# Hybrid pooling and retention trunk on one core: later gate rows as four narrow rows in one bank, biased once and copied to all partitions by DMAs

## The reference

```python
cond = jax.nn.silu(c)
mod = jnp.einsum('bd,sdk->bsk', cond, ada_w[i]) + ada_b[i]
shift_t, scale_t, gate_t = jnp.split(mod[:, 0], 3, axis=-1)
shift_m, scale_m, gate_m = jnp.split(mod[:, 1], 3, axis=-1)
h = modulate(rmsnorm(x, norm_g[i, 0]), shift_t, scale_t)
x = x + gate_t[:, None, :] * y                 # y: pooling or retention of h
h = modulate(rmsnorm(x, norm_g[i, 1]), shift_m, scale_m)
x = x + gate_m[:, None, :] * sq_relu_mlp(h, mlp_w1[i], mlp_w2[i])
```

## Time and profile before

| | |
|---|---|
| time, median of 3 runs | 2412.22 us (2411.78 to 2412.8) |
| span of the profiled execution | 2411.1 us |
| matmuls | 10401 records; PE 2338.8 us busy |
| weights and other data read from DRAM | 616.26 MB |
| mean DMA rate | 257 GB/s |

### The profile page before, as it was taken

One profiled execution on the slowest core, in us unless ns is written; L12 is line 12 of the kernel. 1 busy time (PEld: TensorE's weight loads), 2 busy tenths in 40 slices (PEclk: granted clock), 3 DMA queues, 4 the chain that ended last, 5 costly groups with the idle time before them and its releaser, 6 DMA issues.

```text
span 2411.1 us, 28969 instructions
## 1 busy us (share of the span) xinstructions
PE 2338.8 (97%) x10401; PEld 1856.6 (77%) x10401; DVE 1581.6 (66%) x1655; ACT 1087.5 (45%) x1354; POOL 22.2 (1%) x32
## 2 busy tenths in 40 slices
PE   6689999999999999999999999999999999999998
PEld 2146788888888887878888888887888888888886
DVE  4578887776786787656566657566876545445455
ACT  2324554544534545444444444445543443443443
POOL 0000000000000000000000000000000000000000
PEclk9799999999999999999999999999999999999999
DMA  9999988898888876776667776766986656656654
GB/s 391 405 408 373 335 315 325 308 312 271 299 305 277 300 260 218 239 224 218 218 225 230 237 224 219 225 219 199 333 289 228 187 189 193 185 190 192 188 185 151
DMA packets 269147, 620.28 MB, mean 257 GB/s; under 512 B 19064, under 2 KB 19400, under 8 KB 268112
## 3 DMA queue, kind: packets, MB, share of 16 engines
q1 hardware_dynamic: 267520, 612.44, 75.1%
q0 software_dynamic: 880, 5.77, 0.7%
q10 hardware_dynamic: 608, 0.22, 0.0%
HBM read 616.26 MB, written 2.10 MB: 256 GB/s over the span
## 4 chain that ended last, share of the span: by engine, by line
PE 88%; DMA 5%; DVE 4%; issue 1%; ACT 1%; SPq 0%; POOL 0%; ACTq 0%; POOLq 0%; DVEq 0%
PE acc L556 83%; DMA ada_early_h<-in_ada_w 3%; PE tb L655 2%; DMA raw<-in_mlp_w 1%; DVE ada_acc L1352 1%; DVE w_lo L1346 1%; PE mod_ps L691 1%; DMA ada_raw<-in_ada_w 0%; PE score_ps L905 0%; ACT w_hi L971 0%; PE score_ps L691 0%; SPq L408 0%; DVE h_lo L1540 0%; PE acc L915 0%; PE acc L916 0%
## 5 line engine op out<-in xcount | busy, mean ns | idle before, releaser
L1346 DVE TENSOR_TENSOR w_lo<-raw,w_hi 128x1024 fp32r<-128x1024 f32 x776 | 947.2, 1225 | 724.2 <-ACT w_hi L971 723.8
L971 ACT ACTIVATE w_hi<-raw 128x1024 fp32r<-128x1024 f32 x776 | 821.8, 1060 | 1147.4 <-PE acc L556 1080.9
L556 PE MATMUL acc<-w_hi,h_lo 128*128 128x512 f32 x1792 | 705.6, 394 | 11.9 <-DVE h_lo L1540 5.7
L556 PE MATMUL acc<-w_hi,h_hi 128*128 128x512 f32 x1792 | 698.0, 389 | 0.0
L556 PE MATMUL acc<-w_lo,h_hi 128*128 128x512 f32 x1792 | 697.4, 389 | 0.0
L556 PE MATMUL acc<-w_hi,a_lo 128*128 128x512 f32 x1312 | 516.9, 394 | 0.0
L556 PE MATMUL acc<-w_hi,a_hi 128*128 128x512 f32 x1312 | 511.2, 390 | 0.0
L556 PE MATMUL acc<-w_lo,a_hi 128*128 128x512 f32 x1312 | 511.2, 390 | 0.0
L556 PEld LDWEIGHTS acc<-w_hi,h_lo 128*128 128x128 f32 x1792 | 336.5, 188 | 87.5 <-issue 10.0
L556 PEld LDWEIGHTS acc<-w_hi,h_hi 128*128 128x128 f32 x1792 | 336.4, 188 | 70.6
L556 PEld LDWEIGHTS acc<-w_lo,h_hi 128*128 128x128 f32 x1792 | 336.7, 188 | 69.1 <-issue 1.4
(11 more groups left out here) (164 smaller groups left out, 761.0 us busy)
## 6 DMA issues: line engine op xcount, KB each, us to landing
raw<-in_mlp_w SPq DMA_DIRECT2D x512, 512.0 KB, 4.3
ada_raw<-in_ada_w SPq DMA_DIRECT2D x280, 512.0 KB, 6.0
raw<-in_ret_w_in SPq DMA_DIRECT2D x192, 512.0 KB, 3.9
ada_early_h<-in_ada_w SPq DMA_DIRECT2D x84, 512.0 KB, 13.1
raw<-in_ret_w_out SPq DMA_DIRECT2D x64, 512.0 KB, 4.3
ada_early_a<-in_ada_w SPq DMA_DIRECT2D x20, 512.0 KB, 9.4
raw<-in_pool_w SPq DMA_DIRECT2D x8, 512.0 KB, 13.1
x<-in_x SPq DMA_DIRECT2D x2, 1024.0 KB, 9.8
```

Source lines behind the costliest of these rows:

```text
L556: mm = nc.tensor.matmul(acc[pair][t][:], l[:, CK * c + j, tok], w[:, c % RING, j, :], start=first and j == 0 and i == 0, stop=last and j = ...
L971: nc.scalar.activation(w_hi[:, o % RING], raw[:, o % RING], ACT.Copy).then_inc(hi_ready, 1)
L1346: nc.vector.tensor_tensor(w_lo[:, o % RING], raw[:, o % RING], w_hi[:, o % RING].bitcast(F32), ALU.subtract).then_inc(lo_ready, 1)
```

## The change

A gate of the three is now summed like a shift or scale: `row_sum` after chunk 1 of unit 7, four blocks of 32 columns in `mod_ps`. The bias is loaded by POOL into four rows of `seg_row` (8 KB), DVE adds the bank to `seg_row` once after chunk 3 (128 x 512), and POOL issues four DMAs that each copy one row of `seg_row` (512 floats in partition 0, 32, 64 or 96) to all 128 partitions of a quarter of the target. The waits follow: ACT's next copy to `seg_row`, `mlp_block` in the last group, and the head of `retention()` wait for the copies (`gate_in`, 64 per gate); PE's next sum and the fills of the two banks at a boundary wait for the biased row.

```diff
@@ PE
-            def gate_blocks(b0):
-                if b0 == 0:
-                    pe.wait_ge(ada_done, n.of("AD"))
...
-                pe.wait_ge(gate_ready, n.of("GB"))
-                for b in (b0, b0 + 1):
-                    nc.tensor.matmul((mod_ps, score_ps)[b % 2][:], ones[:], ada_acc[:, b * NB:(b + 1) * NB],
-                                     start=True, stop=True).then_inc(gate_mm, 1)
-                n.add(GB=2)
+            def gate_row_sum():
+                row_sum()
+                n.add(GR=1)
                             if what == "gate" and u == 7:
-                                hooks[1] = [lambda: gate_blocks(0)]
-                                hooks[5] = [lambda: gate_blocks(2)]
+                                hooks[1] = [gate_row_sum]
@@ fill and row_sum, PE
-                    pe.wait_ge(gate_ready, n.of("GB"))
+                    pe.wait_ge(gate_biased, n.of("GR"))
@@ copy_rows, ACT
+                if n.n["GR"]:
+                    act.wait_ge(gate_in, 64 * n.n["GR"])
@@ DVE
-            def take_gate(b0, target, loaded, loads):
-                dve.wait_ge(loaded, 16 * loads)
-                for b in (b0, b0 + 1):
...
-                    nc.vector.tensor_tensor(target[:, blk], (mod_ps, score_ps)[b % 2][:], target[:, blk],
-                                            ALU.add).then_inc(gate_ready, 1)
+            def take_gate_row():
+                dve.wait_ge(row_bias_in, 16 * (n.n["GR"] + 1))
+                dve.wait_ge(row_mm, n.of("RM") + 1)
+                nc.vector.tensor_tensor(seg_row[:], mod_ps[:], seg_row[:], ALU.add).then_inc(gate_biased, 1)
+                n.add(GR=1, RM=1)
                             if what == "gate" and u == 7:
...
-                                hooks[2] = [lambda at=at: take_gate(0, *at)]
-                                hooks[5] = [lambda at=at: take_gate(2, *at)]
+                                hooks[3] = [take_gate_row]
                             if u >= 4 and not last and (layer, first) != (0, 0):
+                                if first == 3 and u == 4:
+                                    dve.wait_ge(gate_in, 64 * (2 * layer + 1))
                                 mlp_block(u % 2, u - 4, first == 0, first == 3)
             def retention():
-                dve.wait_ge(gate_ready, n.of("GB"))
+                dve.wait_ge(gate_in, 64 * 2)
@@ POOL
-            def load_gate_bias(target, norm_, loaded):
-                row = gate_bias[3 * norm_ + 2:3 * norm_ + 3, :].to_broadcast([P, D])
-                pool.dma_start(target, row).then_inc(loaded, 16)
+            def load_gate_bias(norm_, columns):
+                pool.wait_ge(col_T, columns)
+                pool.dma_start(seg_row[0:P:32, :], gate_bias[3 * norm_ + 2].rearrange("(b n) -> b n", b=4)).then_inc(row_bias_in, 16)
+            def spread_gate(target, rows_before):
+                pool.wait_ge(gate_biased, rows_before + 1)
+                for b in range(4):
+                    pool.dma_start(target[:, b * NB:(b + 1) * NB],
+                                   seg_row[32 * b:32 * b + 1, :].rearrange("p (o n) -> p o n", o=1).to_broadcast([1, P, NB])).then_inc(gate_in, 16)
             pool.wait_ge(h_ready, CH)
-            load_gate_bias(mlp_gate, 1, mlp_bias_in)
+            load_gate_bias(1, 4)
+            spread_gate(mlp_gate, 0)
             pool.wait_ge(part_sum, 6 * TT)
-            load_gate_bias(gate[:], 2, ret_bias_in)
+            load_gate_bias(2, 6)
+            spread_gate(gate, 1)
             tile_roots()
...
             pool.wait_ge(x_added, 16 * TT)
-            load_gate_bias(mlp_gate, 3, mlp_bias_in)
+            load_gate_bias(3, 8)
             pool.wait_ge(h_ready, CH + 2 * (2 * CH))
             pool.dma_start(final_gain, final_g.rearrange("(a n) -> a n", a=1).to_broadcast([P, D])).then_inc(final_in, 16)
+            spread_gate(mlp_gate, 2)
             tile_roots()
```

More of the change, by code:

```diff
@@ L60 @@
     NAMES = ("U", "E", "SQ", "XA", "RO", "TB", "TL", "SC", "Y", "AD", "AP", "SG", "RM",
-             "TR", "CS", "GB", "YA", "NO", "GN", "HT", "SB", "MS", "XS", "T0", "PS")
+             "TR", "CS", "GB", "GR", "YA", "NO", "GN", "HT", "SB", "MS", "XS", "T0", "PS")
     def __init__(self):
@@ L283, in program @@
         bias_rows_in = sem("bias_rows_loaded")
-        mlp_bias_in = sem("mlp_gate_bias_loaded")
-        ret_bias_in = sem("ret_gate_bias_loaded")
+        row_bias_in = sem("gate_bias_in_seg_row")
+        gate_biased = sem("gate_row_biased")
+        gate_in = sem("gate_row_spread")
         ret_in = sem("ret_tables_loaded")
@@ L739, in row_sum @@
                 pe.wait_ge(col_used, n.of("CS"))
-                pe.wait_ge(gate_ready, n.of("GB"))
+                if n.of("GR"):
+                    pe.wait_ge(gate_biased, n.of("GR"))
                 row_blocks(mod_ps, 0, 4, True)
+            def gate_row_sum():
+                row_sum()
+                n.add(GR=1)
             def column(bank):
@@ L1243, in group @@
                             n.unit("h1" if half else M_KINDS[u])
+                        if what == "gate":
+                            n.add(RM=1, GR=1)
                     if trips == 1:
@@ L1366, in ada @@
                     dve.wait_ge(row_mm, n.of("RM"))
-                    dve.wait_ge(gate_mm, n.of("GB"))
                 dve.wait_ge(ada_in[a % RING], (ada_round() + (a // RING + 1)) * 16)
@@ L1423, in gate_row @@
                 nc.vector.tensor_tensor(seg_row[:], seg_row[:], scale_row[:], ALU.mult).then_inc(row_ready, 1)
-            def take_gate(b0, target, loaded, loads):
-                dve.wait_ge(loaded, 16 * loads)
-                for b in (b0, b0 + 1):
-                    dve.wait_ge(gate_mm, n.of("GB") + 1)
-                    blk = slice(b * NB, (b + 1) * NB)
-                    nc.vector.tensor_tensor(target[:, blk], (mod_ps, score_ps)[b % 2][:], target[:, blk],
-                                            ALU.add).then_inc(gate_ready, 1)
-                    n.add(GB=1)
+            def take_gate_row():
[3 more added lines that the diff above has]
+                n.add(GR=1, RM=1)
             def take_column(index, bank=mod_ps, b0=0, b1=4):
@@ L1819, in group @@
                             if what == "gate" and u == 7:
-                                at = (mlp_gate, mlp_bias_in, layer + 1) if first == 0 else (gate, ret_bias_in, 1)
-                                hooks[2] = [lambda at=at: take_gate(0, *at)]
-                                hooks[5] = [lambda at=at: take_gate(2, *at)]
+                                hooks[3] = [take_gate_row]
                             elif what and u == 7:
```

## The result

The changed kernel takes 2471.0 us (median of 5 runs, 2468.9 to 2471.7) against 2411.8 (5 runs, 2411.3 to 2412.8): a ratio of 1.0243, with a 95% interval of 1.0233 to 1.0254, or 59.2 us slower. The forecast was 2480.0. The profiled execution is the fastest of the five, with a span of 2466.8 us.

The account below looks back on a forecast made before the run. PE, busy 97% of the span, was taken to bound the kernel. 2412.2 - 6.7 (PE saved) + 27 + 20.5 + 27 (stalls at the three gates) = 2480.0 us, range 2403 to 2500.

Parts of the forecast that it names:

- PE's saving: At each gate, four narrow rows replace two pairs of full-height products: 3.44 - 1.20 = 2.24 us less PE, three gates 6.7.
- The pace of the copies: At each gate, one source partition serves all DMA engines at one engine's pace, 23.9 GB/s: 1.05 MB takes 44 us.
- Why the source is slow: In the gate copies, the read side is a single partition, taken to serve no faster than one engine's share, 23.9 GB/s.
- The loads are held: At gates one and three, loads of w alternate packets with the copies, land 7.7 and 19.3 us late: 27 us stall each.
- The margin: Loads of w after a gate may be 10.6 us late, 14.3 from issue to landing, before PE stalls.
- The second gate: At the head of the retention layer, copies land at 958.5 against 938.0 allowed: PE stalls 20.5 us.
- the wait that I put first: DVE at the head of the retention layer waits for all eight copies so far; held-up loads land within its 20.5 us.
- DVE, bias, POOL's queue: Four DVE additions become one, bias loads shrink to 8 KB, POOL issues take 2.1 to 4.1 us a gate: no effect.
- The root of tile 0: Next in POOL's queue after the second gate's issues, moving from 920.05 to 917.9; fits by 1.8 us at the dear end.
- fast copies: Rival: one partition serves 16 engines in 10 us or less, leaving only PE's 6.7 us gain: 2405.5; chance 0.28.
- slow copies that don't hold the loads: Rival: engines continue loads while awaiting the partition, so only the 20.5 us retention wait costs: 2426.0; chance 0.18.

Follow-up runs that it names:

- wide source: Changed kernel with each of a gate's four copies reading seg_row in all 128 partitions instead of one row 128 times (not the gate's values): 2404.7 us, ratio 0.9967.
- DRAM rows: Changed kernel, but POOL first stores the four rows of seg_row to DRAM and the four copies read them there: 2404.7 us, ratio 0.9972.
- the wait moved: Changed kernel with DVE's wait for the second gate's copies moved from the head of retention to the first block reading the gate: 2469.7 us, ratio 1.0238.
- fewer copies: Changed kernel with two, one and three copies at the three gates instead of four each, leaving part of the gates' values out: 2428.4 us, ratio 1.0072.
- the other order: Changed kernel with a gate's copies issued from partitions 0, 64, 32, 96 instead of 0, 32, 64, 96: 2444.1 us, ratio 1.0134.
- four ports: Changed kernel with bias loaded to all 32 rows of each block and copies reading partitions 0, 36, 72, 108: 2435.9 us, ratio 1.0100.

## Why the prediction was right, step by step

- **PE's saving** (2.24 us a gate): right. The narrow rows take 1.65 us over two steps, and the kernels without stalls (wide source, DRAM rows) are 7.1 to 7.9 us faster than before, against 6.7.
- **The pace of the copies** (one engine's share, 44 us a gate): right in kind, a seventh too long. The last copy lands 38.1 us after the first issue at the first gate (36.5 after its own, which is 1.6 later), 27.5 GB/s instead of 23.9. The estimate from the Trainium skill (SBUF — State Buffer, Door 1: The DMA port swizzle), 38.5 us at 27.2 GB/s for one port, was nearer, and the trace agrees with its figure: all engines together move 27 and 28 GB/s from 420 to 430 us, when the copies from one port have nearly everything.
- **Why the source is slow** (one partition's pace): wrong in the detail. It is the pace of something that partitions 0 and 32 share and 64 does not, by the skill's formula a port; the order of the copies shows it. One partition read without repetition was not run.
- **The loads are held**: right, but not in the way that the prediction worked out. ACT waits up to 28.8 us for a load. The prediction took packets of the two queues in turn, as many bytes for the loads as for the copies: one load after 22 us, the next after 44, and two stalls of 7.7 and 19.3. The Trainium skill (DMA: Bandwidth & Descriptors, Queues, rings and completion order) says too that an engine takes the queues in turn, packet by packet; this trace shows no such sharing while the first copies run. From 420 to 430 us the total of 27 to 28 GB/s leaves the loads next to nothing, the first held load lands after 36.5 us with the last copy, and PE stalls once, 22.3 us. The stall of 27 came out near because both ways end with the last copy.
- **The margin** (14.3 us from issue to landing): right, and better than the step that used it. At the first and third gates PE's stall is the last copy's landing less 13 to 14, since the held load lands with that copy: 36.5 and 22.3, 35.6 and 21.5 in the changed kernel; 36.4 and 23.5, 36.0 and 22.6 with the wait moved; 20.4 and 6.1, 27.0 and 13.1 with fewer copies; 27.5 and 13.7, 27.4 and 13.6 in the other order; 24.7 and 10.5, 23.3 and 9.5 from four ports. The difference is 12.9 to 14.3 in these ten places. The forecast of 27 us was 4.7 too long, the copies' time 5.9.
- **The second gate** (20.5 us): 13.9 measured. The landing at 970.1 is one cause with the held loads; the wait that I put first is hidden by them, as the moved wait shows. Its price was mis-sized with the copies' time.
- **No term for PE's clock**: 1.6, 2.9 and 2.1 us. That it was missing made up by luck for a part of the stalls being too long: 27 + 20.5 + 27 = 74.5 forecast against 57.7 and 6.6. With the clock in the sum the forecast would have been near 2487, further from 2471.
- **DVE, bias, POOL's queue** at nothing: right. The root of tile 0 starts at 938.14, 3.4 us after POOL's last issue, so the copies did not delay it.
- **The rivals**: fast copies were excluded by the landing times; slow copies that don't hold the loads, by ACT's waits for loads at the first and third gate.

## What to carry to other kernels

Spreading a row over all partitions by DMA was cheap here from DRAM or from a source that is itself wide, and ruinous from one partition of SBUF: not for those who wait for the row, but for the loads beside it, since the copies keep all DMA engines busy at 27 to 48 GB/s where the same share moves 324 elsewhere. If a slow transfer can't be avoided, break it into pieces shorter than the margin of the stream beside it. The margin can be read from a trace of the kernel before, and the stall is the transfer's time less that margin.

## What the runs showed of the hardware that I had not expected

- While the first copies run, the loads on SP's queue do not get a share beside them but almost nothing (27 to 28 GB/s in all from 420 to 430 us).
- The order of four equal copies is worth 27 us: 2471 with 0, 32, 64, 96, and 2444 with 0, 64, 32, 96.
- A DMA issue on ACT's or SP's queue can take long while the DMA engines are clogged: up to 10.1 us on ACT, and on SP (issues of `raw` at the first gate of the changed kernel, ns min/median/max) up to 12.6 us:

```profile
L394 SPq DMA_DIRECT2D raw<-in_mlp_w x14: 367/368/12625, 406.7 to 469.9; - x14
```

- PE starts again at 1.2 GHz after each stall: after 22.3 us idle it has 2.4 GHz again 3 us later and loses 1.6; after 13.9 us, 6 us later, and loses 2.9; after 21.5 us, 4 us later, and loses 2.1. The shortest stall cost the most.
